# Feed-forward products of a decoder layer by one level of Strassen's algorithm, with the low part of weight sum S4 on GpSimd

## What is computed

```
D_MODEL, D_FF = 1024, 4096
x = x + CrossAttn(RMSNorm(x), memory K/V)          # ends in the product with w_xo
h = rms_norm(x, norm_ffn_g)
x = x + jnp.square(jax.nn.relu(h @ w_up)) @ w_down
y = rms_norm(x, final_g)
```

## Time and profile before

| what | value |
|---|---|
| time, median of 3 runs | 1443.41 us (1442.57 to 1444.26) |
| span of the profiled execution, first to last instruction | 1441.1 us |
| TensorE busy | 1424.3 us, 99% |
| VectorE busy | 571.1 us, 40% |
| ScalarE busy | 473.2 us, 33% |
| GpSimd busy | 414.3 us, 29% |
| HBM traffic | 79 GB/s over the span |

### The profile page before, as it was taken

One profiled execution on the slowest core, in us unless ns is written; L12 is line 12 of the kernel. 1 busy time (PEld: TensorE's weight loads), 2 busy tenths in 40 slices (PEclk: granted clock), 3 DMA queues, 4 the chain that ended last, 5 costly groups with the idle time before them and its releaser, 6 DMA issues.

```text
span 1441.1 us, 22538 instructions
## 1 busy us (share of the span) xinstructions
PE 1424.3 (99%) x9509; PEld 1395.9 (97%) x9509; DVE 571.1 (40%) x644; ACT 473.2 (33%) x634; POOL 414.3 (29%) x324
## 2 busy tenths in 40 slices
PE   7999999999999999999999999999999999999997
PEld 7999999997999999899999999999999999999997
DVE  5639998885533655523322111221112211122124
ACT  7662354457524343312332101321003210032224
POOL 6545492227122211012222222222222222222220
PEclk9999999999999999999999999999999999999999
DMA  8511250112524211861111111111111111111113
GB/s 341 168 52 54 57 53 30 42 33 67 228 92 166 98 45 45 285 228 45 44 45 44 59 44 44 44 44 59 44 44 44 44 58 44 44 44 44 45 43 118
DMA packets 47455, 114.12 MB, mean 79 GB/s; under 512 B 7768, under 2 KB 23448, under 8 KB 45984
## 3 DMA queue, kind: packets, MB, share of 16 engines
q1 hardware_dynamic: 47392, 113.22, 24.8%
HBM read 100.90 MB, written 12.30 MB: 79 GB/s over the span
## 4 chain that ended last, share of the span: by engine, by line
PE 96%; ACT 2%; DVE 1%; issue 0%; DMA 0%; SPq 0%; DVEq 0%; ACTq 0%
PE ps L1305 60%; PE ps L1418 16%; PE ps L1712 6%; PE ps L1435 3%; PE m L1386 2%; PE ps L1746 1%; PE ps L1665 1%; PE m L1625 1%; PE ps L1845 1%; PE ps L1725 1%; PE m L1689 1%; PE m L1638 1%; PE ps L1656 0%; PE m L1540 0%; DVE x_res L2432 0%
## 5 line engine op out<-in xcount | busy, mean ns | idle before, releaser
L676 POOL TENSOR_TENSOR w_split<-w_raw,w_split 128x512 fp32r<-128x512 f32 x230 | 313.8, 1385 | 964.8 <-ACT w_split L765 964.7
L1305 PE MATMUL ps<-a_op,w_split 128*128 128x344 f32 x3168 | 499.4, 319 | 0.0
L1305 PEld LDWEIGHTS ps<-a_op,w_split 128*128 128x128 f32 x3168 | 497.8, 188 | 0.5 <-issue 0.5
L1305 PE MATMUL ps<-b_op,w_split 128*128 128x344 f32 x2304 | 362.3, 319 | 0.0
L1305 PEld LDWEIGHTS ps<-b_op,w_split 128*128 128x128 f32 x2304 | 361.7, 188 | 0.0
L1418 PE MATMUL ps<-a_op,w_split 128*128 128x344 f32 x1440 | 232.8, 321 | 0.0
L1418 PEld LDWEIGHTS ps<-a_op,w_split 128*128 128x128 f32 x1440 | 226.6, 188 | 0.4
L765 ACT ACTIVATE w_split<-w_raw 128x1024 fp32r<-128x1024 f32 x116 | 121.7, 1050 | 261.8 <-PE ps L1305 246.0
L2010 DVE SCALAR_TENSOR_TENSOR ps<-conv_in,par,ps 128x1024 f32<-128x1024 f32 x103 | 133.0, 1291 | 3.3
L2374 DVE SCALAR_TENSOR_TENSOR tmp<-ps,rstd 128x1032 f32<-128x1032 f32 x32 | 39.5, 1233 | 211.0 <-PE ps L1305 203.2
L2384 DVE TENSOR_TENSOR x_res<-x_res,ps 128x1032 f32 x24 | 29.5, 1230 | 230.8 <-PE ps L1305 230.8
(11 more groups left out here) (266 smaller groups left out, 1122.3 us busy)
## 6 DMA issues: line engine op xcount, KB each, us to landing
w_raw<-in_wt SPq DMA_DIRECT2D x117, 512.0 KB, 3.5
cache_b<-in_cache_v SPq DMA_DIRECT2D x8, 1024.0 KB, 11.9
...
```

Source lines behind the costliest of these rows:

```text
L676: gp.tensor_tensor(split(t, slot)[:, 1, part, :], src, split(t, slot)[:, 0, part, :].bitcast(F32), ALU.subtract).then_inc(w_low_done, 1)
L1305: last = pe.matmul(ps[:, c0 // CB, 0:w], w_split[:, slot, wp, k, :], src[:, k, xp, c0:c0 + w], start=(k == 0 and j == 0), stop=(k == KT - ...
```

## The change

The hidden layer and x are cut into 2x2 blocks, and each block product into Strassen's seven products (Winograd's form) in place of eight. The tokens are taken in two halves of HT = 516, each of two quarters of Q = 258; a step is a pair of weight tiles (p and p + 4 of a group), whose halves make the 2x2 block A11, A12, A21, A22 of pieces 128 x 512. There are 64 steps (2 halves x 4 groups x up/down x 4 pairs), so each weight is loaded and split twice. A step has seven products of 4 pieces x 3 matmuls x 258 columns. The last step is done plainly, in blocks of 258, 172 and 86 columns.

Per step, weight side: GpSimd forms S1 = A21 + A22, S2 = S1 - A11, S3 = A11 - A21, S4 = A12 - S2 from the raw weights (`comb_sum`); ScalarE copies seven high parts (`comb_top`); the low parts of A11, S2, S1, S3 are subtracted on VectorE and those of A12, A22, S4 on GpSimd (`comb_low`). They go to a ring of 8 slots that come free one by one as products finish. Per step, result side: ScalarE copies the first product out of PSUM, VectorE makes five sums (`add_first`, `add_second`, `add_c22`, `add_c12`, `add_c21`). An up step then has the ReLU and square on ScalarE, the sums T1 to T4 of the hidden blocks on VectorE (`hidden_sums`, `hidden_last_sum`), the high part of the 7 factors on ScalarE and the low part, 7 x 258 = 1806 columns, on VectorE (`hidden_low`). A down step adds to x_res three times (`x_first`, `x_second`, `x_rest`). The factors of the norm's output (`factors`, `factor_rest`) are made once for each half, so now rstd is applied ahead of the products. The final norm of the first half is worked into steps 36 to 54 (`final_add`, `final_scale`). The w_xo tiles 2 to 7 are cut into token halves too (12 half tiles of 48 matmuls of 258 columns), and the feed-forward block is written out in full, without loops.

```diff
+STEPS = [(half, g, kind, p) for half in range(2) for g in range(FG) for kind in ("up", "down") for p in range(KT // 2)]
+COMBOS = ("A11", "S2", "S1", "S3", "A12", "S4", "A22")
+HIGH_ORDER = ("A11", "S2", "A12", "S1", "S3", "A22", "S4")
+DVE_LOWS = ("A11", "S2", "S1", "S3")
+POOL_LOWS = ("A12", "A22", "S4")
+FACTOR = (B11, T2, T1, T3, B21, B22, T4)
+BANK = (0, 1, 2, 3, 0, 2, 3)
...
+        def wait_comb_free(eng, c):
...
+            else:
+                eng.wait_ge(product_done, c - 7)
...
-            with gp.Fori((T_OUT + 3) // 2, N_T // 2) as i:
-                lo(i * 2, 0)
-                lo(i * 2 + 1, 1)
...
+            def comb_low(s, name):
+                wait_comb_high(gp, s, name)
+                c = comb(comb_of(s, name))
+                gp.tensor_tensor(c[:, 1], comb_low_from(s, name), c[:, 0].bitcast(F32), ALU.subtract).then_inc(comb_low_pool, 1)
+
+            for s in range(N_ST):
...
+                wait_raw(gp, s, "A21")
+                wait_comb_free(gp, comb_of(s, "S1"))
+                comb_sum(s1, raw_part(s, "A21"), raw_part(s, "A22"), ALU.add)
+                wait_raw(gp, s, "A11")
+                gp.wait_ge(comb_sums, 4 * s + 1)
+                if s >= 1:
+                    wait_comb_low(gp, s - 1, "S2")
+                comb_sum(s2_raw[:, :, :], s1, raw_part(s, "A11"), ALU.subtract)
+                wait_comb_free(gp, comb_of(s, "S3"))
+                comb_sum(s3, raw_part(s, "A11"), raw_part(s, "A21"), ALU.subtract)
+                comb_low(s, "A12")
+                wait_comb_free(gp, comb_of(s, "S4"))
+                gp.wait_ge(comb_sums, 4 * s + 2)
+                comb_sum(s4, raw_part(s, "A12"), s2_raw[:, :, :], ALU.subtract)
+                comb_low(s, "A22")
+                comb_low(s, "S4")
...
+            def product(s, i, ks=range(KT // 2)):
...
+                weights = comb(comb_of(s, COMBOS[i]))
+                for k in ks:
+                    factor_wait(s, i, k)
+                    for j, (wp, xp) in enumerate(((0, 0), (0, 1), (1, 0))):
+                        last = pe.matmul(SETS[s % 2][BANK[i]][:, 0:Q], weights[:, wp, k, :], op[:, k, xp, FACTOR[i], :],
...
+            for s in range(LAST_STEP):
+                kind, p = STEPS[s][2:]
+                after_up = s >= 1 and STEPS[s - 1][2] == "up"
+                if s >= 1:
+                    add_c21(s - 1)
+                    if not after_up:
+                        x_rest(s - 1)
...
+                add_first(s)
+                comb_low(s + 1, "A11")
+                add_second(s)
+                if after_up and p:
+                    hidden_low(s - 1, "all")
...
+                add_c22(s)
+                comb_low(s + 1, "S2")
+                comb_low(s + 1, "S1")
...
+                if kind == "down":
+                    x_first(s)
+                add_c12(s)
+                if kind == "down":
+                    x_second(s)
+                elif p == 3:
+                    hidden_low(s, "first")
+                comb_low(s + 1, "S3")
```

More of the change, by code:

```diff
@@ new lines, in _ @@
+            for j in range(5):
+                residual_half(j)
+            residual_half(5)
+            norm_half(0)
+            residual_half(6)
+            factor_high(0, 0)
+            residual_half(7)
+            residual_half(8)
+            factor_high(0, 1)
+            residual_half(9)
+            factor_high(0, 2)
+            residual_half(10)
+            comb_top(0, "A11")
+            factor_high(0, 3)
+            residual_half(11)
+            for name in HIGH_ORDER[1:6]:
+                comb_top(0, name)
@@ new lines, in half_sums @@
+            def half_sums(banks, src):
+                for b in range(2):
+                    pe.matmul(banks[b][:, 0:Q], ones[:, :], src(b), start=True, stop=True).then_inc(sums_ready, 1)
+            for j in range(XO_HALVES):
+                if j == KT - 2:
+                    xo_half(j, range(0, 4))
+                    pe.wait_ge(squares_summed, 19 + KT - 2)
+                    half_sums(M, lambda b: acc[:, Q * b:Q * (b + 1)])
+                    xo_half(j, range(4, KT))
+                else:
+                    xo_half(j, range(KT))
@@ new lines, in _ @@
+            for s in range(LAST_STEP):
+                if STEPS[s][3] == 0 and STEPS[s][2] == "down":
+                    product(s, 0)
+                    for i in (1, 2, 3):
+                        product(s, i, range(0, 3))
+                    for i in (1, 2, 3):
+                        product(s, i, range(3, 4))
+                elif s in (0, N_ST // 2):
+                    for i in range(4):
+                        product(s, i, range(0, 3))
+                    for i in range(4):
+                        product(s, i, range(3, 4))
+                else:
+                    for i in range(4):
+                        product(s, i)
+                product(s, 4)
+                if s == 0:
+                    pe.wait_ge(ps_free, T_SPLIT)
+                    pe.wait_ge(squares_summed, 19 + XO_HALVES)
+                    half_sums((PS[1][:, 0, :], PS[1][:, 1, :]), lambda b: acc[:, HT + Q * b:HT + Q * (b + 1)])
+                if s == NORM_STEP:
+                    wait_c11_read(pe, s - 1)
+                    pe.wait_ge(c_step, 5 * (s - 1) + 4)
+                    pe.wait_ge(squares_summed, E_SUMS)
+                    idle = SETS[(s + 1) % 2]
+                    half_sums((idle[0], idle[2]), lambda b: f_sum[:, b, :])
+                product(s, 5)
+                product(s, 6)
@@ L1873, in _ @@
+            pe.matmul(M[0][:, 0:Q], ones[:, :], e_acc[:, 0:Q], start=True, stop=True).then_inc(sums_ready, 1)
+            end_block(1, 1, range(0, KT))
+            end_block(0, 2, range(0, KT))
+            pe.wait_ge(squares_summed, E_SUMS + 9)
             for j, c0 in enumerate(END_GROUPS[1]):
-                last = pe.matmul(M[1][:, j:j + 1], acc[:, c0:c0 + P], ones[:, 0:1], start=(j == 0), stop=(j == 2))
+                last = pe.matmul(M[1][0:END_W, j:j + 1], e_acc[:, c0:c0 + END_W], ones[:, 0:1], start=(j == 0), stop=(j == 1))
@@ L1886, in _ @@
[L1886 to L1888 removed]
+            pe.wait_ge(sums_read, 14)
+            pe.wait_ge(squares_summed, E_SUMS + 10)
+            c0 = END_GROUPS[2][0]
+            pe.matmul(M[0][0:END_W, 0:1], e_acc[:, c0:c0 + END_W], ones[:, 0:1], start=True, stop=False)
+            pe.wait_ge(square_done, E_SQUARES + 12)
+            pe.matmul(M[0][0:END_W, 0:1], e_sq[:, 1, c0:c0 + END_W], ones[:, 0:1], start=False, stop=True).then_inc(sums_ready, 1)
@@ new lines, in _ @@
+            factors(0, 0)
+            residual_half(KT - 1)
+            factor_rest(0, 0)
+            factors(0, 1)
+            residual_half(KT)
+            factor_rest(0, 1)
+            factors(0, 2)
+            residual_half(KT + 1)
+            factor_rest(0, 2)
+            factors(0, 3)
+            residual_half(KT + 2)
+            factor_rest(0, 3)
+            comb_low(0, "A11")
+            residual_half(KT + 3)
+            for name in DVE_LOWS[1:4]:
+                comb_low(0, name)
```

747 lines of the change are left out of this document (555 added, 192 removed).

## The result

The changed kernel took 1607.6 us in the median of 4 runs (1606.0 to 1609.2) against 1443.4 us before: 1.114 times the time of before, 95% interval 1.112 to 1.115. The forecast of 1577 us (1495 to 1650) had the direction right, the measured time lies inside its range, and its size was 31 us low. The profiled execution, one of the four, spans 1607.5 us for the 1441.1 of before.

A forecast was written before the change was run, and what follows sets the result against it. GpSimd, slowed by exclusion with VectorE's two-SBUF-input operations, was to replace TensorE as the bound: 702 + 786 + 23 + 35 + 3 + 17 + 8.6 = 1575 us of span, so 1577 us, range 1495 to 1650.

The forecast's parts named there:

- the start: Before step 0: GpSimd forms three sums ahead of w_xo's end, so its 63 steps count from about 702 us.
- the switch: Change to the second token half: VectorE's operations for four factors cost GpSimd 3.53 us each, 14 us in all.
- the right 0.45 us: Feed-forward steps: a 512-column VectorE operation with two SBUF inputs adds 0.45 us to GpSimd's time.
- the 11.46 of the sum: Down steps: GpSimd's own 9.03 us plus 2.43 us of exclusion by VectorE make 11.46 us a step.
- the full charge: Feed-forward steps: GpSimd loses VectorE's whole operation, 3.87 us down and 6.34 up; 116 us more, 1693 us.
- The first rival: Feed-forward steps: TensorE stays the bound because exclusion costs GpSimd under 0.92 us a step; faster, 1368 us; chance 9%.
- the third rival: Feed-forward steps: VectorE becomes the bound from a mean wait of 0.73 us; 1663 us at 1.0 us; chance 14%.
- GpSimd's step is 13.46 up: Up steps: GpSimd sets the pace, its own 9.03 us plus 4.43 us of exclusion by VectorE.
- The price of S4's place: S4's low part in 63 steps: 1.275 us on GpSimd, 0.45 of GpSimd's time if on VectorE; worth 52 us.
- the coupling: Passages from up to down and turn-taking in up steps: engines waiting for each other, 35 us, bounds 0 and 60.
- cutting the w_xo tiles changes nothing: w_xo tiles before the feed-forward block: cut into halves, TensorE's matmuls take 68.2 us for 67.8.
- The clock: Feed-forward steps: TensorE's clock falls for want of work; folded into the upper end of the range; chance 1%.

The follow-up runs named there:

- all_reduce: Against the changed kernel, VectorE's two-SBUF-input operations in the steps became one-element reductions (wrong numbers), GpSimd's seven operations kept; 1439.8 us.
- pool_memset: Against the changed kernel, GpSimd's seven operations of each step became memsets of the same tiles, which read nothing from SBUF; 1418.1 us.
- start_lean: Against the changed kernel, first-half factors' low parts come one factor later on VectorE and their operations take one input (wrong numbers); 1601.3 us.
- no_pool: Against the changed kernel, GpSimd's seven operations of a step moved to VectorE for steps 1 to 62, same result; 1517.1 us.

## Why the prediction was right, and where it was off

- **The mechanism is shown.** Exclusion between VectorE's two-input operations and GpSimd costs at least 168 us (all_reduce, which keeps it at the start and the switch); without it in the steps the change comes out 4 us under the kernel before. The single meetings of the earlier trace rows gave the right 0.45 us. In down steps GpSimd is full, and the 11.2 to 11.4 us are the 11.46 of the sum.
- **Charged 0.45 us, not the whole operation.** With the whole of VectorE's operation charged the forecast's sum gave 1693. The 1.73 to 1.76 us of GpSimd's operations in full queues agree with 0.45, so the trace of before decided rightly against the full charge. For the 1806 columns the sum had 1.82 us, and 1.74 was measured.
- **TensorE.** 12 matmuls of 258 columns take 1.44 us, 120 ns for the 118.4 of the forecast, 10.08 us a step: nothing as long as TensorE isn't the bound. The first rival's 1368 us was too low: the two kernels in which TensorE did set the steps took 1418 and 1440. The pace explains 63 x 0.13 = 8 us of that; the rest is the late start below, the passages and the switch.
- **Who is the bound.** Two of the signs that I gave came out: TensorE near 80% (83%), and steps of 12.5 to 13 us (102.4/8 = 12.8, without the switch and the norms). Three didn't: GpSimd over 90% busy (85%), its mean of 1.7 to 1.8 us (1.66), and TensorE waiting for low parts of the weights, where it waits for VectorE's sums. In up steps the third rival's sign holds, VectorE without idle time and GpSimd with gaps, at a mean wait of 0.74 us, on its threshold of 0.73. So the step "GpSimd's step is 13.46 up" had the wrong queue: GpSimd's seven operations took 12.56 us there, and the 13.67 are VectorE's thirteen, 14.38 less 0.71 of overlap. That the two numbers lie so close is luck. (The rival's 907 us for a wait of 1.0 us should be 31 x 12.4 + 32 x 16.4 = 909.) The price of S4's place was wrong: the step "on VectorE it would cost GpSimd 0.45, so its place is worth 52 us" counted GpSimd's side alone, where VectorE had no room left, and it was 5 us.
- **The mis-sized terms.** TensorE's last step began at 1578.06, for 702 + 786 + 58 + 3 = 1549 in the sum: 29 us late. Of these 6 lie between step 0 and step 62: the intervals add up to 838.7 us, for 32 x 13.46 + 30 x 11.46 + 58 = 832.5. There the coupling was 22 us and not 35 (seven times 102.4 and 80.0 for the last six, less 774.5), and all that lies above the regular pace, switch and norms, 42 and not 23, the switch alone 26 for 14. The other 23 us are the start, which the sum had at 702. The last step and the end took 29.4 us for 25.6.
- **The start.** GpSimd's first sum began late, and then stood behind ScalarE. VectorE's, GpSimd's and TensorE's rows of the changed kernel:

```profile
700.72 2.88 DVE L2799 TENSOR_TENSOR u_op<-u_f,u_op 128x1806 fp32r<-128x1806 f32 x1 [1.86 <-ACT u_op L1460]
703.52 1.53 DVE L2791 SCALAR_TENSOR_TENSOR u_f<-x_res,par,rstd 128x516 f32<-128x516 f32 x2
...
715.36 1.39 POOL L915 TENSOR_TENSOR comb_a<-w_raw 128x512 f32<-128x512 f32 x1 [3.85 <-DMA w_raw<-in_wt]
...
726.91 1.36 POOL L920 TENSOR_TENSOR comb_a<-w_raw,comb_a 128x512 fp32r<-128x512 f32 x1 [7.32 <-ACT comb_a L1472]
...
710.42 7.53 PE L2146 MATMUL ps<-a_op,w_split 128*128 128x258 f32 x48 [3.79 <-POOL w_split L853]
724.58 2.30 PE L2203 MATMUL ps<-u_op,comb_b 128*128 128x258 f32 x9 [6.63 <-DVE comb_b L2809]
```

  The forecast had the first sum at 702 and w_xo's end at 704.7, as in the earlier trace rows. But each of the last half tiles of w_xo, 5.7 us on TensorE, now has a factor's operations on VectorE behind its residual add (at 700.72 to 703.52 in these rows), about 10 us with the waits: the step "cutting the w_xo tiles changes nothing" looked at TensorE alone. The first sum is 13 us late, and its weights' load only starts behind w_xo's last split. start_lean, with these operations shortened, had its first sum 4.4 us earlier (710.95 us); that the rest has the same cause is read from the trace and not tried. The next wait, 7.32 us, is most of the rest. The fills of pool_memset moved step 0 by only 3 us, start_lean by 6: exclusion against the sums is a small part of it. How the remaining 14 us divide stays open.
- **The switch.** Its surplus is 26 us with exclusion, 24 in all_reduce, which left the factors of the second half as they were, and 9 in pool_memset. So where VectorE has room the factors' meetings with GpSimd make 15 us of it. But no_pool, in which VectorE is full and meets nobody, has 22 us as well (112.6 less 90.5). I had charged GpSimd's side, 14 us; in the changed kernel the switch is VectorE's, which works 34.08 of the 34.7 us from 1116.5 us on, GpSimd 24.56. How its 26 us divide into own work and meetings no run shows.
- **The clock.** I gave it 1%. Windows of the changed kernel in a passage, and TensorE's rows in the same stretch:

```profile
792.00:794.00 2.00, 0.29 (x3) 0.16 (x1) 2.00 (x3) 0.00 (x0) 1.87 (x2) 0.79 0.00 0
794.00:800.00 6.00, 6.00 (x28) 6.00 (x29) 5.33 (x8) 2.89 (x6) 5.68 (x4) 0.50 0.00 0
800.00:804.00 4.00, 4.00 (x35) 4.00 (x34) 3.67 (x4) 1.47 (x4) 3.03 (x2) 1.00 0.00 0
...
793.87 5.50 PE L2203 MATMUL ps<-d_op,comb_b 128*128 128x258 f32 x24 [1.71 <-issue]
```

  It fell to 0.50, the 1.2 GHz level, for some 6 us after TensorE had stood still for 1.7 us, and 24 matmuls took 5.50 us for 2.9. It came back while TensorE worked without a gap. Such falls lie at all eight passages, in the switch and in some up steps; over the 63 steps the mean granted clock is 0.94. Since the engines that set the pace are others, it need not cost what it takes from TensorE; no run here separates its cost.
